# Latent attention of a float32 transformer kernel: keys and queries made for pairs of heads, rotary parts together, output weights split inside the head loop, and two steps reordered

## What is computed

```python
# cd layer; z = h @ cd_w_in, split into f_in, f_gate, cq (256), ckv (128), kr (32), d_gate
q  = (rms_norm(cq) @ w_q_up).reshape(L, 8, 64 + 32)       # 8 heads: 64 plain, 32 rotary columns
q  = concat([q[..., :64], axial_rope(q[..., 64:])])
kv = (rms_norm(ckv) @ w_kv_up).reshape(LA, 8, 64 + 64)    # LA = 512 tokens + 256 of the context
k  = concat([kv[..., :64], broadcast(rope(kr))])          # one rotary part for all heads
p  = softmax(q @ k.T * 96 ** -0.5)                        # 8 heads, 512 x 768
attn = p @ kv[..., 64:]
y = concat([(fft2(f_in).real @ w_f) * silu(f_gate), attn * silu(d_gate)]) @ w_out
x = layer_norm(ALPHA * x + gate * y)
```

## Time and profile before

| | |
|---|---|
| three runs | 2903.94, 2907.4, 2909.63 us (median 2907.4) |
| profiled execution | 2907.38 us, of which the span of its instructions 2905.6 us |
| granted TensorE clock, mean | 0.969 |
| TensorE busy | 2769.2 us (95%) |
| VectorE, ScalarE, GpSimd busy | 1162.3, 957.5, 143.4 us |
| DMA | 250.06 MB, mean 86 GB/s |

### The profile page before, as it was taken

One profiled execution on the slowest core, in us unless ns is written; L12 is line 12 of the kernel. 1 busy time (PEld: TensorE's weight loads), 2 busy tenths in 40 slices (PEclk: granted clock), 3 DMA queues, 4 the chain that ended last, 5 costly groups with the idle time before them and its releaser, 6 DMA issues.

```text
span 2905.6 us, 34955 instructions
## 1 busy us (share of the span) xinstructions
PE 2769.2 (95%) x14803; PEld 2216.7 (76%) x14803; DVE 1162.3 (40%) x1735; ACT 957.5 (33%) x1429; POOL 143.4 (5%) x261
## 2 busy tenths in 40 slices
PE   7999999997999999997999999999999997999998
PEld 5877776566888888774788888888888774788887
DVE  3313652555433234455533324333244445533322
ACT  2222332442222225455332223322234445322211
POOL 0040000000000001001100000000001001100000
PEclk8999999999999999998999999999999997999999
DMA  9521240001323223110223322333223110222221
GB/s 302 180 89 44 73 129 27 25 1 66 114 90 102 102 87 92 44 59 30 73 88 101 102 94 86 111 102 102 90 87 90 54 49 30 73 95 92 97 102 73
DMA packets 208048, 250.06 MB, mean 86 GB/s; under 512 B 6399, under 2 KB 187222, under 8 KB 207894
## 3 DMA queue, kind: packets, MB, share of 16 engines
q1 hardware_dynamic: 207894, 247.83, 26.0%
HBM read 245.72 MB, written 2.10 MB: 85 GB/s over the span
## 4 chain that ended last, share of the span: by engine, by line
PE 87%; DVE 5%; ACT 3%; issue 2%; DMA 1%; SPq 1%; POOL 1%; DVEq 0%; POOLq 0%; ACTq 0%
PE psum L781 84%; PE psum L1243 1%; PE psum L1164 1%; PE psum L851 1%; ACT w_hi L1403 1%; SPq L662 0%; DVE w_lo L1809 0%; DMA mod_w<-in_ab_w_mod 0%; DVE spare_lo L1809 0%; DVE h_lo L1818 0%; POOL stats_first L2413 0%; DVE stats_first L1885 0%; DVE work L1878 0%; ACT softplus L1761 0%; ACT softplus L1763 0%
## 5 line engine op out<-in xcount | busy, mean ns | idle before, releaser
L781 PE MATMUL psum<-h_hi,w_hi 128*128 128x512 f32 (+1 forms) x2096 | 786.6, 375 | 6.6 <-ACT v_a L1412 4.1
L781 PE MATMUL psum<-h_lo,w_hi 128*128 128x512 f32 (+1 forms) x2096 | 779.3, 372 | 0.0
L781 PE MATMUL psum<-h_hi,w_lo 128*128 128x512 f32 (+1 forms) x2096 | 779.0, 372 | 0.0
L1809 DVE TENSOR_TENSOR w_lo<-raw,w_hi 128x2048 fp32r<-128x2048 f32 (+1 forms) x176 | 400.4, 2277 | 800.2 <-ACT w_hi L1403 799.8
L781 PEld LDWEIGHTS psum<-h_hi,w_hi 128*128 128x128 f32 x2096 | 398.6, 190 | 81.4 <-issue 15.0
L781 PEld LDWEIGHTS psum<-h_hi,w_lo 128*128 128x128 f32 x2096 | 397.7, 190 | 68.1
L781 PEld LDWEIGHTS psum<-h_lo,w_hi 128*128 128x128 f32 x2096 | 398.5, 190 | 66.3 <-issue 0.5
L1403 ACT ACTIVATE w_hi<-raw 128x2048 fp32r<-128x2048 f32 (+1 forms) x176 | 332.8, 1893 | 223.2 <-PE psum L781 217.7
L781 PE MATMUL psum<-w_hi,ff_hi 128*128 128x512 f32 x576 | 224.7, 390 | 0.0
L781 PE MATMUL psum<-w_lo,ff_hi 128*128 128x512 f32 x576 | 224.2, 389 | 0.0
L781 PE MATMUL psum<-w_hi,ff_lo 128*128 128x512 f32 x576 | 224.2, 389 | 0.0
(11 more groups left out here) (287 smaller groups left out, 3248.1 us busy)
## 6 DMA issues: line engine op xcount, KB each, us to landing
raw<-in_ffn_w_gate SPq DMA_DIRECT2D x44, 1024.0 KB, 5.2
raw<-in_ffn_w_up SPq DMA_DIRECT2D x44, 1024.0 KB, 5.2
raw<-in_ffn_w_down SPq DMA_DIRECT2D x44, 1024.0 KB, 4.8
raw<-in_w_in SPq DMA_DIRECT2D x36, 512.0 KB, 5.1
raw<-in_ab_w_in SPq DMA_DIRECT2D x10, 1024.0 KB, 7.7
mod_w<-in_ab_w_mod SPq DMA_DIRECT2D x8, 1024.0 KB, 11.8
raw<-in_w_out SPq DMA_DIRECT2D x8, 1024.0 KB, 4.8
raw<-in_cd_w_in SPq DMA_DIRECT2D x7, 1024.0 KB, 5.5
```

Source lines behind the costliest of these rows:

```text
L781: return pe.matmul(o, lhsT, rhs, start=start, stop=stop, skip_group_check=True)
L1809: dve.tensor_tensor(lo[:, 0:nk * n], raw[c % 2][:, 0:nk * n], hi[:, 0:nk * n].bitcast(F32), ALU.subtract).then_inc(*w_lo_made.mark(key))
```

## The change

1. **Order, late product 14.** `late(14)` is requested ahead of the eighth projection chunk.
2. **Order, gate rows.** `gate_diags` and `gate_row` of the cd layer move from chunk 1 to chunks 6 and 7.
3. **Weights laid out apart.** The up-projections of queries and of keys and values are loaded as four tiles by 24 DMAs in all with the rotary constants (before: five DMAs); the pieces are 32 or 64 columns wide. SyncE first waits for a GpSimd memset of `swap`.
4. **Rotary parts together.** The rotary columns of all eight heads are made as two products of 128 columns (`q_rope`, 4 heads each) and turned with two `swap` products, ahead of and within the Fourier mix. The key's rotary part is turned in four copies at once.
5. **Pairs of heads.** Keys and queries of two heads come out of one product of 128 columns. Four `kT` and four `qT` tiles hold them, with 32 rows of zeros so that odd heads contract over 128 rows. The pairs 1 to 3 are made in rounds n % 8 = 1 and 3; VectorE copies the rotary rows in (two copies of 32 rows, n % 8 = 5).
6. **Values, first keys and queries** move ahead of the two `fnet` chunks.
7. **Output weights.** Chunks 1, 2 and 3 of `w_out` are split in rounds 4, 27 and 29 (`CD_SPLITS`), and SyncE requests the first two feed-forward chunks before the attention ends.

```diff
+CD_SPLITS = (None, 4, 27, 29)
...
-            raws_to(7)
             late(14)
+            raws_to(7)
...
+            sp.wait_ge(*swap_zeroed["all"])
+            for i in range(4):
+                at = rows_of(i)
+                for k in range(2):
+                    sp.dma_start(q_turn[:, k, :, ROPE_AT[i], :], q_heads[k][:, i::4, NOPE:QK]).then_inc(*mla_landed.mark("q_rope"))
+                sp.dma_start(rope_c[at, :], A["k_rope_cos"][NOPE:QK, :]).then_inc(*mla_landed.mark("rope"))
...
...
-            raws_to(CHUNK["cd", 0] + 2)
+            raws_to(CHUNK["cd", 0] + 5)
...
-                    if ch == 1:
+                    if ch == 7:
                         gate_row(("gate_cd", j))
...
+            def pair_keys(p):
+                for r, (off, n) in enumerate(RANGES):
+                    b = claim(rot.take(), ("keys", p, r))
+                    done(mm(bank(b, n), k_up[:, p * P:(p + 1) * P], ckvT[:, off:off + n], True, True), ("keys", p, r))
...
-                if n < len(seq) and seq[n][0] + 1 < HEADS and seq[n][1] in beside:
-                    beside[seq[n][1]](seq[n][0] + 1)
+                if n < len(seq) - 8 and n % 8 == 1:
+                    pair_keys(n // 8 + 1)
+                if n < len(seq) - 8 and n % 8 == 3:
+                    pair_queries(n // 8 + 1)
...
+                if n in CD_SPLITS:
+                    split_at(CHUNK["cd", 0] + CD_SPLITS.index(n))
```

More of the change, by code:

```diff
@@ L1107, in tensor_program, with pair_queries @@
                 done(m, ("spec", hd))
+            for t in range(6):
+                b = claim(rot.take(), ("vall", t))
+                done(mm(bank(b), ckvT[:, t * P:(t + 1) * P], v_up[:, :], True, True), ("vall", t))
+            def pair_keys(p):
+                for r, (off, n) in enumerate(RANGES):
+                    b = claim(rot.take(), ("keys", p, r))
+                    done(mm(bank(b, n), k_up[:, p * P:(p + 1) * P], ckvT[:, off:off + n], True, True), ("keys", p, r))
+            def pair_queries(p):
+                b = claim(rot.take(), ("queries", p))
+                for k in range(2):
+                    m = mm(bank(b), q_nope[:, k, p * P:(p + 1) * P], cqT[:, k, :], k == 0, k == 1)
+                done(m, ("queries", p))
+            pair_keys(0)
+            pair_queries(0)
             for c in range(2):
@@ L1591, in over_features @@
                     copy(f_cs[hd % 2][:, t, :], event, full(event, 256), f_cs_made, (hd, t))
+            for blk in range(2):
+                copy(q_rope[:, blk, :], ("qr", blk), full(("qr", blk)), q_made, ("rope", blk))
             over_features(0)
@@ L1597, in scalar_program, with pair_keys, pair_queries @@
                 split_hi_of(("spec", hd), spec_hi[:, hd, :], full(("spec", hd)), psum_full["spec", hd])
+            act.wait_ge(*rope_step["rope", "kr"])
+            for i in range(4):
+                at = rows_of(i)
+                act.activation(kT[i][at, :], krT[at, :], ACT.Copy).then_inc(*keys_shared.mark(i))
+            for t in range(6):
+                event = ("vall", t)
+                copy(v_all[:, t, :], event, full(event), v_made, t)
+            def pair_keys(p):
+                if p > 1:
+                    act.wait_ge(*psum_full["scores", 2 * p - 3, NT - 1, 0])
+                for r, (off, n) in enumerate(RANGES):
+                    event = ("keys", p, r)
+                    for hd in (2 * p, 2 * p + 1):
+                        p0 = 64 * (hd % 2)
+                        copy(kT[hd % 4][p0:p0 + NOPE, off:off + n], event, rows(event, p0, p0 + NOPE, n), k_made, (hd, r))
+                    freed[event] = k_made[hd, r]
+            def pair_queries(p):
+                event = ("queries", p)
+                for hd in (2 * p, 2 * p + 1):
+                    p0 = 64 * (hd % 2)
+                    copy(qT[hd % 4][p0:p0 + NOPE, :], event, rows(event, p0, p0 + NOPE), q_made, hd)
+                freed[event] = q_made[hd]
+            pair_keys(0)
+            pair_queries(0)
             for c in range(2):
```

179 lines of the change are left out of this document (97 added, 82 removed).

## The result

The changed kernel takes 2890.8 us (median of four runs, 2890.1 to 2891.6) where the kernel before takes 2906.9 (2903.9 to 2909.6): a ratio of 0.9942, 95% interval 0.9927 to 0.9958. So it is 16 us faster, and I had forecast 37, with a range that ends at 2884. The direction was right, the size was not. One execution of one kernel among the experiments (3906.5 us, mean granted clock 0.649) was a slow run and is left out of every figure.

The account below looks back on a forecast made before the run. TensorE was taken to set the end wherever it has work. Terms -10.7 - 8.9 + 1 + 0.2 - 19.4 + 9.6 + 5 - 14.3 = -37.5 gave 2870 us; own range 2863 to 2877, widened to 2857 to 2884.

Parts of the forecast that it names:

- Loads of the attention's weights: 24 requests instead of 5 ahead of chunk 6, with 2.8 us of slack: +1 us, ends 0 and 5.
- Small packets are dear: Rival: short packets cost 30 ns each, chunk 6 is 5 us late, clock falls once more (2): 2876 to 2878; chance 0.14.
- the ends that I gave for the open terms: Unknown terms at their ends, -1 +4, -2.4 +3, and -5 +1 on the clock, said to give 2863 to 2877.
- Late product 14: Requesting its weights ahead of a projection chunk closes a 6.78 us TensorE hole and the low clock behind it: -10.7 us.
- Gate rows: Moving them out of chunk 1 brings the context's transpose 10.6 us earlier; two products come back in chunk 7: -8.9 us.
- First transposes and loop together: Up to the first transposed probabilities +0.2, head loop -19.4, splits inside it +9.6 and their low clock +5 us.
- The waits behind the splits: In the head loop, w_hi then w_lo delay the row maximum; TensorE waits behind rounds 4, 27, 29: +9.6, clock +5 us.
- The output: With w_out already split, chunks 1 to 3 follow at once and VectorE's norm starts at 671.9 instead of 686.25: -14.3 us.
- the upper end of my sum: Short packets take 4.7 to 9.3 us over 16 DMA engines; by the skill's page nearer the upper end, some 4 us more.

Follow-up runs that it names:

- The kernel with the pieces: Kernel before with q_up and kv_up loaded in pieces of 32 and 64 columns by six requests instead of two: 2906.9 us against 2909.1, ratio 0.9990.
- the last, 2855.5: Changed kernel with chunk 6 requested before the small loads, w_hi and w_lo splits in different rounds, and an early exponential written into mod_sum: 2855.5 us, ratio 0.9821.
- chunk 6 first: Changed kernel with chunk 6 of cd_w_in requested ahead of the 24 small loads, nothing else moved: 2872.5 us.

## Why the prediction was wrong

**The step that failed** is "Loads of the attention's weights", +1 with ends of 0 and 5, and its rival "Small packets are dear", 6 above the forecast. It cost 16.9: a wait of 4.45, which lies inside my ends, and 12.4 of low clock behind it, for which the sum has nothing. Two things were wrong within it.

First its size. I counted what the DMA engines do with the packets and not what SyncE does with the requests; the queue of the kernel before, just ahead of the request in the earlier trace rows, would have told:

```profile
406.23 0.51 SPq L713 DMA_DIRECT2D q_up<-in_cd_w_q_up  x1
406.78 0.47 SPq L714 DMA_DIRECT2D kv_up<-in_cd_w_kv_up  x1
```

At such a price 19 more requests are already some 9 us. The queue held chunk 6 back 12.8 us, and its landing moved by 5.9 against the 1 to 5 that I gave; of these, 2.4 go with the short packets and 3.5 with the number of requests, which no term had. The slack was 1.7, not 2.8, since the want came 3.2 nearer and not 2.1.

Second, and nearly three times as dear, its consequence: in the rival I priced the low clock behind a wait there at 2 us, as if it were the output's. It was 12.4. I had rows at 512 and 256 columns (3.9 us behind late product 14, 1.9 in the output), none at 160, and took the nearest number instead of asking what work follows. This price stood in no bound, and so the range ended 7 us too low. (The range has a small slip too: the ends that I gave for the open terms add up to -8.4 and +8, that is 2861.5 and 2878, not 2863 and 2877. It changes nothing here.)

**What held.** Late product 14: -10.7 against -10.9 in the trace, -9.2 alone. Gate rows: -8.9 against -9.0 in the trace, though between 4 and 5 of it are lost again in the second block. First transposes and loop together: -4.6 against -5.5. The waits behind the splits, 3.5, 3.5 and 2.6, were 3.19, 3.19 and 2.24, by the chain that I named; with their clock 11.6 against 14.6. The output: -14.3 against -14.2. The kernel with the pieces puts the short packets at 2.4 us of landing, inside the 1 to 5 that I took from the rows. The Trainium skill ("DMA: Bandwidth & Descriptors", Specifications) says that transfers under 512 bytes are read, modified and written. The 2.4 us neither prove nor exclude that mechanism; they are not at the upper end of my sum, where I had put the Trainium skill's rule.

**What no step had.** The ab stage and the second block gave back 3.5 and 5.3 us by low clocks behind waits that both kernels have. 4.6 of the 5.3 come from one place, a wait of 1.14 in the token mixing, after and before:

```profile
1206.00:1212.00 6.00, 6.00 (x24) 3.15 (x22) 1.64 (x3) 2.07 (x4) 0.00 (x0) 0.50 0.01 3
```

```profile
1226.00:1232.00 6.00, 6.00 (x44) 4.31 (x43) 3.21 (x6) 2.70 (x7) 0.00 (x0) 1.00 0.00 0
```

The same instructions behind the same wait, at 0.50 in one and 1.00 in the other. The 17 traces have a pattern here: the three kernels with the gate rows in chunk 1 (before, late product 14 alone, the pieces) keep the upper level behind this wait, and of the 14 kernels that move them all but one (the last, 2855.5) lose it; behind the same wait in the second layer of the block all 17 lose it. So what the gate rows bring is in good part lost here. What links the two is not shown, and I found nothing in the profile that tells in advance which it will be. A few such places may well make the 9 to 15 us by which the runs of the kernel before differ within one series; that is argued, not shown. With chunk 6 first, at 2872.5, the forecast of 2870 would have stood in spite of them, by the luck told above.

## What to carry to other kernels

Price a wait by its length and by what rows show for the work behind it: here the low clock behind waits of 2.8 to 7.1 us cost 2 to 4 us ahead of products of 256 and 512 columns, and behind one of 4.7 it cost 12 ahead of a row of 160 columns; filling that wait with useless products saved 14.7, halving it some 4. Count what a queue of requests does to the next request that matters, and put that one first; here the small loads had time. Where an operation on two engines has to go into the slack of a tight loop, give each engine's half its own round.

## What was not expected of the hardware

- A clock that fell behind a wait stayed at 0.50 for 26 us of work without a gap (418 to 444) while the products had 160 columns, and was back some 4 us after those of 512 began (0.80 in the window from 442 to 448). The same products ran at 1.00 with a wait of 0.38 ahead of them, and with none.
- The fall is not a fixed consequence of the wait: of two waits of 3.19 us in one execution one drew it (transposes 1.51 us) and one did not (0.84); and a wait of 1.14 drew it in 13 traces of 17.
- Six requests with some 6100 packets of 128 and 256 bytes held SyncE for 10 us, single ones for 3.5, while 2 MB were on their way and the DMA engines were full (share 1.13); the chunk behind them then took 5.5 us to land instead of 13.6.
- One more small tile in SBUF changes TensorE's pace: 396 ns a product instead of 390 for those of the down weights with `ff_hi` and `ff_lo`, with a tile of 4 bytes as with one of 64. What in the layout this hangs on stayed open.
